# Norm sums taken up beside the chunks, router logits with the tokens moving, and expert gathers that begin at the picks

## The reference, cut to what matters

```
for i in range(2):
    sh1, sc1, g1, sh2, sc2, g2 = split(silu(c) @ mod_w[i] + mod_b[i], 6)
    x = x + g1 * mixer_i(modulate(rmsnorm(x, norm1_g[i]), sh1, sc1))
    h = modulate(rmsnorm(x, norm2_g[i]), sh2, sc2)
    x = x + g2 * expert_choice_ffn(h, router_w[i], w1[i], w3[i], w2[i])
return rmsnorm(x, final_norm_g)

# expert_choice_ffn: 16 experts, each takes its 32 best tokens of a stream of 256
# affinity = softmax(h @ router_w); picks = top 32 tokens of every expert
# y = (silu(h_picked @ w1) * (h_picked @ w3)) @ w2; out[token] += affinity * y
```

## Time and profile before

| | us |
|---|---|
| median of three timed runs (2467.17 to 2472.73) | 2470.86 |
| the profiled execution | 2471.49 |
| its span, first to last instruction | 2469.8 |
| PE busy / DVE / ACT / POOL | 2008.5 / 778.9 / 496.9 / 189.6 |
| chain that ended last: PE / DMA / DVE | 51% / 28% / 9% |
| of it the expert weights `in_moe_w` | 26% |
| mean granted TensorE clock | 0.913 |

### The profile page before, as it was taken

The page is one execution under the profiler, slowest core; times in us unless marked ns, Lnnn a source line. Parts: engine busy times, 40 slices in busy tenths (PEclk is TensorE's granted clock), DMA queues, the critical chain, the costliest instruction groups (busy, mean ns, idle before and its releaser), DMA issues.

```text
span 2469.8 us, 30766 instructions
## 1 busy us (share of the span) xinstructions
PE 2008.5 (81%) x12656; PEld 1061.9 (43%) x12656; DVE 778.9 (32%) x1454; ACT 496.9 (20%) x1037; POOL 189.6 (8%) x230
## 2 busy tenths in 40 slices
PE   5998869977699699888987998979998856566565
PEld 2444634444344523333323655657787722122111
DVE  2112643357701300100003774757765110000001
ACT  2233312222201200000002422244443200000000
POOL 0000000032100000000003100025541000000000
PEclk9998989999999699999999998989998868878777
DMA  9013022150012389999997136210001369999995
GB/s 371 26 68 136 0 96 75 68 204 0 10 64 98 136 377 428 431 432 429 430 431 309 69 142 253 91 69 2 2 3 69 137 254 431 430 429 432 432 431 239
DMA packets 57503, 527.15 MB, mean 213 GB/s; under 512 B 2848, under 2 KB 4128, under 8 KB 43040
## 3 DMA queue, kind: packets, MB, share of 16 engines
q1 hardware_dynamic: 55760, 522.55, 50.9%
q10 hardware_dynamic: 1616, 2.76, 0.3%
HBM read 524.26 MB, written 1.05 MB: 213 GB/s over the span
## 4 chain that ended last, share of the span: by engine, by line
PE 51%; DMA 28%; DVE 9%; issue 3%; ACT 3%; DVEq 2%; PEld 1%; SPq 1%; PEldq 1%; ACTq 0%; POOL 0%
DMA ring<-in_moe_w 26%; PE bank L469 19%; PE bank L962 10%; PE bank L894 5%; PE bank L862 2%; DVE ring L1709 2%; PE bank L574 1%; PE bank L643 1%; PE bank L666 1%; DMA ring<-in_cd_w 1%; PE bank L440 1%; DVE x L2126 1%; DMA ring<-in_ab_w 1%; PE bank L951 1%; PE bank L905 1%
## 5 line engine op out<-in xcount | busy, mean ns | idle before, releaser
L469 PE MATMUL bank<-hT,ring 128*128 128x512 f32 (+1 forms) x1504 | 554.6, 527 | 24.2 <-DMA ring<-in_cd_w 12.9
L962 PE MATMUL bank<-ring,xgs 128*32 128x512 f32 x3072 | 393.1, 667 | 145.8 <-DMA ring<-in_moe_w 144.4
L469 PEld LDWEIGHTS bank<-hT,ring 128*128 128x128 f32 x1504 | 286.5, 193 | 272.7 <-issue 239.8
L962 PEld LDWEIGHTS bank<-ring,xgs 128*32 128x32 f32 x3072 | 108.4, 121 | 406.9 <-issue 296.1
L962 PE MATMUL bank<-ring,hT 128*32 128x512 f32 x1536 | 208.8, 701 | 82.8 <-DMA ring<-in_moe_w 82.8
L1948 DVE SCALAR_TENSOR_TENSOR x<-bank,modT,x 128x256 f32<-128x256 f32 x96 | 42.2, 480 | 477.2 <-PE bank L986 477.2
L962 PEld LDWEIGHTS bank<-ring,hT 128*32 128x32 f32 x1536 | 57.8, 125 | 221.2 <-issue 170.1
L1937 DVE TENSOR_TENSOR hT<-sils,bank 128x512 f32<-128x512 f32 x24 | 15.8, 685 | 409.2 <-PE bank L962 409.2
L1566 DVE SCALAR_TENSOR_TENSOR x<-gluR,cols,x 128x256 f32<-128x256 f32 x240 | 116.0, 483 | 16.0 <-issue 0.4
L1354 ACT ACTIVATE sils<-bank 128x512 f32<-128x512 f32 x24 | 13.5, 595 | 425.3 <-PE bank L962 425.3
L894 PE MATMUL bank<-mixA,ring 128*128 128x512 f32 x128 | 58.6, 612 | 7.9 <-DVEq L2085 7.7
(11 more groups left out here) (442 smaller groups left out, 2452.4 us busy)
## 6 DMA issues: line engine op xcount, KB each, us to landing
ring<-in_moe_w SPq DMA_DIRECT2D x96, 4096.0 KB, 22.4
ring<-in_mod_w SPq DMA_DIRECT2D x48, 1024.0 KB, 11.7
ring<-in_cd_w SPq DMA_DIRECT2D x6, 4096.0 KB, 20.3
ring<-in_ab_w SPq DMA_DIRECT2D x5, 4096.0 KB, 21.7
ring<-in_ab_wo SPq DMA_DIRECT2D x2, 4096.0 KB, 15.7
ring<-in_cd_wo SPq DMA_DIRECT2D x2, 4096.0 KB, 12.9
x<-in_xT SPq DMA_DIRECT2D x1, 2048.0 KB, 10.5
ring<-in_ab_w SPq DMA_DIRECT2D x1, 2048.0 KB, 15.6
```

Of the source, the lines that this page charges most:

```text
L469: last = mm(ps[p["no"] % 4][:, p["c0"]:T], w[:, k, :], hT[:, k, p["c0"]:T], start=(k == 0), stop=(k == KD - 1))
L962: last = mm(ps[banks + s][32 * j:32 * j + 32, :], lhs[s][:, 4 * kh + k, 32 * j:32 * j + 32], w[:, j, k, :], start=(kh == 0 and k == 0), st ...
```

## The change

- Norms 1 to 4 no longer start after the whole of `x` is ready. In the out projections DVE squares each chunk right after adding it, and PE adds the sum of chunk c - 1 (`norm_sum`) after the product of chunk c. Since `hT` now holds squares, ACT's scaled result goes to other buffers (`out_scaled_at`). In the last scatter of each layer's experts ACT squares each chunk as it is added, and PE puts the sum of chunk dt - 2 behind scatter step dt. Norms 2 and 4 sum in bank 0, since the scatter uses bank 7.
- In layer 0 the modulation's products stand as before behind the norm, but the turning of its row moves behind the turning of the logits, and DVE's part behind the affinities.
- The logits are computed with the 16 router columns stationary and all tokens moving, chunk by chunk as `h_ready` rises. The result (16 x 512) is copied to SBUF by DVE and turned by one small transpose for each tile. The first tile of tokens is turned while DVE copies.
- Gathers go half by half, stream within half. PE no longer waits for `routed`; the gathers of the first half start after the first `picks`, and product 0 follows them. The other gathers and the turning of the gates (bank 5 and 6) stand behind products 0 and 1 of the first pass. `routed` is waited for at the first scatter.
- The output leaves in two DMAs of four chunks each.

```diff
@@ out projections (both), PE
+                    norm_sum(1, c - 1, T)
+                norm_sum(1, 7, T)
@@ norm_sum, PE
+            def norm_sum(i, k, cw):
+                if k < 0:
+                    return
+                pe.wait_ge(sg("norm_squared"), 8 * (i - 1) + k + 1)
+                last = mm(norm_bank(i)[:, 0:cw], ones[:, :], hT[:, k, T - cw:T], start=(k == 0), stop=(k == KD - 1))
+                if k == KD - 1:
+                    last.then_inc(sg("norm_sums"), 1)
@@ route, PE
-                for t in tiles:
-                    for k in range(KD):
-                        last = mm(ps[0][:, E * t:E * t + E], hT[:, k, t * P:(t + 1) * P], router[:, k, :],
+                for k in range(KD):
+                    pe.wait_ge(sg("h_ready"), 8 * (2 * layer + 1) + k + 1)
+                    last = mm(ps[0][0:E, c0:T], router[:, k, :], hT[:, k, c0:T], start=(k == 0), stop=(k == KD - 1))
+                last.then_inc(sg("logits"), 1)
+                turn_tokens(0, tiles[0])
+                pe.wait_ge(sg("logits_copied"), layer + 1)
+                for t in tiles:
+                    last = nc.tensor.transpose(ps[3][:, E * t:E * t + E], lgT[:, t * P:(t + 1) * P], ident[0:E, 0:E])
+                last.then_inc(sg("logits_turned"), 1)
+                if layer == 0:
+                    modulation_turn(1, 0)
-                pe.wait_ge(sg("htok_copied"), 8 * layer + 2 * len(tiles))
-                pe.wait_ge(sg("picks"), 2 * layer + 2)
-                (16 or 8 transposes of pgate)
@@ experts, PE
-                for b in range(4):
+                pe.wait_ge(sg("picks"), 2 * layer + 1)
+                pe.wait_ge(sg("htok_copied"), 8 * layer + 4 * ns)
+                for b in range(ns):
                     gather(0, b)
                     product(q, 0, 0, xg[q % 2], 0)
                     scatter(q - 1, (0, 1))
+                    if q == 0:
+                        for b in range(ns, 2 * ns):
+                            gather(0, b)
+                        turn_gates(0)
+                        turn_gates(1)
+                    pe.wait_ge(sg("moe_xg"), gathered(layer, streams, q + 1, 0))
                     product(q, 1, 1, xg[q % 2], 0)
                     scatter(q - 1, (2, 3))
+                    if q == 0:
+                        turn_gates(2)
+                        turn_gates(3)
-                scatter(Q - 1, range(KD))
+                for dt in range(KD):
+                    scatter(Q - 1, (dt,))
+                    norm_sum(2 + 2 * layer, dt - 2, 256 * ns)
@@ order of PE's program
-            norm(1, T)
-            modulation(1, 0)
-            pe.wait_ge(sg("h_ready"), 2 * KD)
+            modulation_rows(1, 0)
             route(0, (0, 1))
-            pe.wait_ge(sg("routed"), 1)
             experts(0, (0, 1))
-            norm(2, T)
@@ experts, ACT, at the end
+                for dt in range(KD):
+                    act.wait_ge(sg("moe_added"), 8 * (Q * layer + Q - 1) + dt + 1)
+                    A_(hT[:, dt, cc], x[:, dt, cc], ACT.Square).then_inc(sg("norm_squared"), 1)
@@ out projection, DVE
+                    last = V.tensor_tensor(x[:, c, cc], x[:, c, cc], out_scaled_at(layer, c)[:, cc], ALU.add).then_inc(sg("out_added"), 1)
+                    dve.drain()
+                    V.tensor_tensor(hT[:, c, cc], x[:, c, cc], x[:, c, cc], ALU.mult).then_inc(sg("norm_squared"), 1)
                 dve.drain().then_inc(sg("x_ready"), 1)
@@ final, DVE
+                    if k % 4 == 3:
+                        dve.drain().then_inc(sg("out_ready"), 1)
```

More of the change, by code:

```diff
@@ L380, in _ @@
                 load_group(sp, n, stage, i)
-            sp.wait_ge(sg("out_ready"), 1)
-            sp.dma_start(out.rearrange("(k p) t -> p k t", p=P), hT[:, :, SEQ:T]).then_inc(sg("out_written"), 16)
-            sp.wait_ge(sg("out_written"), 16)
+            for half in range(2):
+                sp.wait_ge(sg("out_ready"), half + 1)
+                sp.dma_start(out.rearrange("(k p) t -> p k t", p=P)[:, 4 * half:4 * half + 4, :],
+                             hT[:, 4 * half:4 * half + 4, SEQ:T]).then_inc(sg("out_written"), 16)
+            sp.wait_ge(sg("out_written"), 32)
         @block.tensor
@@ L979, in scatter @@
                     done = Q * layer + q
+                    if q == 0 and steps[0] == 0:
+                        pe.wait_ge(sg("routed"), layer + 1)
                     for dt in steps:
@@ L988, in scatter, with turn_gates @@
                         last.then_inc(sg("moe_sum"), 1)
-                for b in range(4):
+                def turn_gates(u):
+                    if u >= 2 * len(streams):
+                        return
+                    s, half = streams[u // 2], u % 2
+                    pe.wait_ge(sg("picks"), 2 * layer + 2)
+                    if u >= 2:
+                        pe.wait_ge(sg("gates_copied"), 4 * layer + u - 1)
+                    for r in range(2):
+                        for tt in range(2):
+                            last = nc.tensor.transpose(ps[5 + half][:, 256 * r + P * tt:256 * r + P * tt + P],
+                                                       pgate[:, s, tt, (2 * half + r) * P:(2 * half + r + 1) * P], ident[:, :])
+                    last.then_inc(sg("gates_turned"), 1)
+                ns = len(streams)
+                pe.wait_ge(sg("picks"), 2 * layer + 1)
+                pe.wait_ge(sg("htok_copied"), 8 * layer + 4 * ns)
+                for b in range(ns):
                     gather(0, b)
@@ L1077, in norm @@
                     act.wait_ge(consts_in, 48)
-                else:
-                    act.wait_ge(sg("x_ready"), i)
-                for k in range(KD // 2):
-                    A_(hT[:, k, T - cw:T], x[:, k, T - cw:T], ACT.Square).then_inc(sg("norm_squares"), 1)
+                    for k in range(KD // 2):
+                        A_(hT[:, k, T - cw:T], x[:, k, T - cw:T], ACT.Square).then_inc(sg("norm_squares"), 1)
                 act.wait_ge(sg("norm_ms"), i + 1)
@@ L1324, in out_projection @@
                         cc = slice(s * SEQ, (s + 1) * SEQ)
-                        last = A_(hT[:, c % 2, cc], ps[c % 4][:, cc], ACT.Identity, bias=gbias[:, c, s:s + 1], scale=mod(layer, 2, c, s))
+                        last = A_(out_scaled_at(layer, c)[:, cc], ps[c % 4][:, cc], ACT.Identity, bias=gbias[:, c, s:s + 1], scale=mod(layer, 2, c, s))
                     last.then_inc(sg("out_scaled"), 1)
@@ L1892, in route @@
                 dve.drain().then_inc(sg("affinities"), 1)
+                if layer == 0:
+                    modulation(1, 0)
                 dve.wait_ge(sg("aff_turned"), 2 * layer + 1)
```

68 lines of the change are left out of this document (35 added, 33 removed).

## The result

The changed kernel takes 2441.12 us, the median of four runs (2437.49 to 2442.07), against 2471.56 of the kernel before in the same session. The ratio is 0.987 with a 95% interval of 0.9859 to 0.9882. The profiled execution took 2442.07 us, its span 2440.3, the mean granted clock is 0.924 instead of 0.913. The two profiled spans are 29.5 us apart, the medians 30.4.

The account below looks back on a forecast made before the run. Bound: the uncovered path to product 0's end, where the weight loads restart. Gains of 16.2 (layer 0), 2.8, 3.4 (layer 1), 1.7 and 1.5 make 25.6 us off 2471.5: forecast 2446, 8-in-10 range 2434 to 2454.

Parts of the forecast that it names:

- The bound: Expert stages end a fixed time after their weight loads restart, so the path from out projection through product 0 counts.
- Rival D: Restart of the loads does not set the experts' end; only the tails count, 6.0 us, giving 2465.5; chance 0.05.
- E: Rival: PE becomes the bound in layer 0's experts and the kernel gets slower, 2487 at ten low-clock groups; chance 0.03.
- Norm sums, layer 0: Out projection of layer 0: sums interleaved with chunks end at 797.1 instead of 800.1, gain 3.0 us.
- Router: Layer 0's router weights, issued at 796.2, land late at 810.8 and hold back the logits.
- Rival B: Router weights come in time in both layers, 15 us better than the forecast, 2431; chance 0.15.
- Logits: Layer 0: eight products take 9.1 us, logits end at 819.9 instead of 829.6, gain 9.7; top-k starts 7.3 later.
- Gather at the picks: Layer 0: gates leave the path, two low-clock gathers take 7.8 us; product 0 ends at 852.5, gain 18.2.
- Rival C: Low clock lasts through both first products and the router lands later than 812: 2450 to 2455; chance 0.15.
- Given back: Layer 0: gathers and gate turns make products 0 and 1 11.7 us apart; the load stream starves 2.0 once.
- Layer 1: Path to the end of layer 1's product 0: 1996.5 instead of 1999.9, gain 3.4 us, though the logits lose 1.2.
- Tails: After the experts: layer 0's scatter and sums gain 2.8 us, the final ones 1.7, the split output 1.5.

Follow-up runs that it names:

- e4: Changed kernel with gates turned, `routed` waited for and all four gathers done ahead of product 0, as before the change; 2453.28 us.
- e2: Kernel before the change, with only the router weights loaded early, ahead of each mixer's scan; 2466.15 us.
- e5: Changed kernel with PE's norm sums behind the last chunk and the last scatter step, squares still chunk by chunk; 2430.48 us.
- e3: Changed kernel with logits computed the old way (tokens stationary, 16 router columns moving), router weights still late; 2448.58 us.
- e10: Changed kernel with the output in one DMA again instead of two; 2444.93 us, one execution.
- e1: Changed kernel with each layer's router weights loaded early into unused tiles, ahead of the mixer's scan; 2426.52 us.
- e6: e1 plus matmuls of no use that keep PE busy while DVE picks tokens and after the turn of the picks; 2424.59 us.
- e9: e1 with logits computed the old way (tokens stationary, 16 router columns moving); 2448.97 us.

## Why the prediction was right, step by step

The time of 2441.1 lies in the range, 4.9 us under the forecast, and the mechanism was the forecast's, not a rival's.

- **The bound.** Right. Each expert stage lasts a nearly fixed time from its first product (460 to 464, and 452 to 455, in thirteen traces), so what precedes product 0 passes through in full. Rival D is refuted by that and by e4, where product 0 came 9.9 and 6.3 us later in its stage and the experts behind it were only 2.3 shorter; E is refuted by the same lengths. Product 0 ended at 851.5 (852.5 predicted).
- **Norm sums, layer 0.** Predicted 3.0. From the projection's start to the end of the sums it is 121.6 us instead of 124.6, so 3.0. In e2, whose code here is that of the kernel before, it is 123.6, so 1 us of the 3.0 may be drift. The six sums ahead of the last chunk cost PE 5.0 us (5.3 predicted). The step was right on what the edit does against the kernel before and silent on what it costs against its own alternative: squares chunk by chunk with sums behind is better by 10.6 (e5), 1.5 of it by the earlier end of the sums and most of the rest by way of the router and the clock behind it. No run took the early squares out.
- **Router.** Issue 797.3 (796.2 predicted), landing 14.6 us later (14.6 predicted), at 811.9 (810.8). The 3 us that I added, for the gap between the loads that closes, came out to the tenth, and the tenth is luck: e3, e4 and e10 have 13.6, 14.4 and 14.3. The gap itself is borne out by six traces. In the kernel before the next 4 MB load goes out 2.2 us after the load beside the router has landed, in e5 1.7 ahead of that, and the router lands with that load (801.8 against 801.7, 804.3 against 804.1). In the changed kernel, e3, e4 and e10 the next load goes out 5.0 to 5.2 ahead of that landing, and the router lands 3.8 to 4.7 behind it. No run changed the gap alone. Rival B is wrong for this kernel, while its price of 15 us was right: e1 measures 14.6. The Trainium skill (DMA: Bandwidth & Descriptors, Anatomy of one DMA) fits the time of a DMA that GpSimd issues, and an estimate from that fit is some 2.2 us for 64 KB. The router's is issued by ACT; e1 shows 1.7 us where the engines are quiet and 8.2 where they are not (below).
- **Logits.** 9.94 us long (9.1, though the third of the time at the low level that I wrote down gives 8.5), top-k start 6.6 behind their end (7.3). From the projection's start, top-k begins 9.7 us earlier, as predicted.
- **Gather at the picks.** The term that was mis-sized. 18.2 was predicted for product 0's end in all, and it is 20.5, counted from the projection's start. The first two gathers took 5.39 us, not 7.8: the clock rose while they ran (0.50, 0.58, 1.00).

```profile
838.00:840.00 2.00, 1.61 (x7) 1.61 (x8) 1.88 (x4) 0.00 (x0) 0.00 (x0) 0.50 0.00 0
840.00:842.00 2.00, 2.00 (x13) 2.00 (x12) 0.92 (x2) 0.00 (x0) 0.00 (x0) 0.58 0.00 0
842.00:844.00 2.00, 1.77 (x16) 1.58 (x15) 0.00 (x0) 0.79 (x2) 0.00 (x0) 1.00 0.00 0
```

I had taken both wholly at the low level, though the earlier trace rows already showed the clock on its way up inside the gathers of the kernel before. In the other kernels that gather at the picks and leave PE idle ahead of it, they took 5.4 to 6.3 us, so up to 0.9 of this is luck. Rival C, that the low clock lasts, didn't happen in layer 0.
- **Given back.** 11.65 us from product 0 to product 1 (11.7 predicted), and the stage is 2.2 longer (2.0). In the other kernels that keep this order it is 2.3 to 3.8, so my 2.0, which counted only the gap itself, lies below them all. Where the rest comes from stays open.
- **Layer 1.** Predicted 3.4, measured 6.2 (8.3 to product 0, 2.1 given back to the slower product 0 and the split). Three sizes were off, none in kind. The interleaved projection is 1.1 us longer, not 2.8. Its clock stood at 1.00 from the start, in the kernel before at 0.50 for the first 3 us, and that is luck: in e3, e6 and e9 it began at 0.50 to 0.56, and the same projection took 1.3 us more. The router landed after 11.0, not 11.4. Logits, the steps to the gather and the gather were 5.00, 13.7 and 3.78 us, not 5.6, 14.4 and 4.0. These three sum to 1.5. So the logits end 1.2 earlier than before, counted from the projection's start, where I had booked 1.2 later. Product 0 took 5.38, where I had 5.0.
- **Tails.** 14.6 us for scatter and sums (14.4), 8.1 for the last ones (7.9; the terms that I wrote down add up to 7.7), 1.6 for the output (1.5). The root follows the table load within 0.01 us (2429.92 + 1.28 and 2431.21), and DVE's result was there at 2431.11, so the load sticks out by 0.1. The Trainium skill (ScalarE: Activation LUTs, What ACT_TABLE_LOAD costs) states a longer switch, of which I had made 1.4 us more. It isn't seen: the load took 1.28 us, and the engine waited neither ahead of it nor behind it.

In sum: 25.6 predicted, plus 2.3 ahead of product 0 in layer 0, 2.8 in layer 1 and 0.4 between layer 0's experts and layer 1's projection, less 1.3 for the later start, 0.2 more given back and 0.1 at the end: 29.5, the difference of the two spans. At least 1.3 us of it (layer 1's projection) is the clock's luck.

## What to carry to other kernels

When a cover is made shorter, list every transfer that ended under it: here a 64 KB load that nobody had waited for became the thing everyone waited for, and issuing it earlier was worth half as much again as the whole change. Before interleaving work into an engine that is already full, ask which signal rides on the end of that stretch and what latency the work filled where it stood. A stage that lasts a fixed time from its first step should be entered with as little as possible, but with enough behind the first step that the second isn't late.

## What was not expected of the hardware

The same 64 KB transfer took 1.7 to 14.6 us to land, by what else the DMA engines carried. For e1 the two landings (layer 1's tile and layer 0's) and the two stretches around their issue:

```profile
DMA to landing us min/median/max: 1.7/1.7/1.7
```

```profile
DMA to landing us min/median/max: 8.2/8.2/8.2
```

```profile
1605.00:1608.00 3.00, 3.00 (x4) 0.67 (x2) 2.31 (x11) 2.97 (x10) 0.66 (x2) 0.50 0.09 25
511.00:520.00 9.00, 5.01 (x20) 2.67 (x17) 4.50 (x7) 0.60 (x1) 4.74 (x4) 0.82 1.01 421
```

At a DMA share of 0.09 it landed in 1.7 us, at 1.01 in 8.2. So a queue of its own doesn't spare a small transfer the time of the large ones beside it, though it need not wait for their end: in e1 it was issued at 511.5 and landed at 519.7, while a 4 MB load issued at 507.9 landed at 525.7. And a wait shortened on PE brought more than its own length, since the next work ran at the higher clock: the logits took 7.40 us at a clock of 1.00 without an idle stretch ahead. Behind one of 6.5 us they took 9.94, at 0.50 until 816 and 1.00 from 818 on, and behind one of 6.3 us 8.4 (e4 and e10).
